# One core, a two-layer denoise step: u's reordering and two loads of Y move from GpSimd's queue to the sync engine's

## The reference, cut to what matters

```python
u, z = split(h @ w_in)                        # 2048 -> 2 x 2048
h_t  = a * h_(t-1) + B u_t                    # complex scan over 128 rows, both directions, 128 groups of 16 channels
y    = gelu(C h + d_skip * u)
y    = y * sigmoid(y @ w_glu + b_glu)
x    = x + gate * ((y * silu(z)) @ w_out)
```

## Time and profile before

| | us |
|---|---|
| median of 3 runs | 1235.92 |
| the three runs | 1229.36, 1235.92, 1236.2 |
| the profiled execution's own time | 1229.89 |
| its span | 1228.1 |

### The profile page before, as it was taken

How to read it: one execution, slowest core, us unless ns; L and a number is a source line. 1 busy time by engine, 2 the same in 40 slices (tenths; PEclk the granted TensorE clock), 3 DMA queues, 4 the chain that set the end, 5 groups by cost and what they waited for, 6 DMA issues and landing times.

```text
span 1228.1 us, 17478 instructions
## 1 busy us (share of the span) xinstructions
PE 1111.2 (90%) x6802; PEld 840.4 (68%) x6802; DVE 766.0 (62%) x1302; ACT 571.1 (47%) x802; POOL 215.5 (18%) x386
## 2 busy tenths in 40 slices
PE   3899998999999999998999979999688977799995
PEld 0356776777777776787777657788577756587884
DVE  4246764766576657666788664299586884365664
ACT  5233443343444344445433454664858466344443
POOL 2001220333022402130322131311010210100000
PEclk9698999999999999999999979999798999899998
DMA  9999785889798978864898867686373946754551
GB/s 355 421 401 398 245 322 196 331 319 345 274 337 323 349 275 328 320 230 174 316 341 339 307 248 272 192 278 227 120 233 120 292 140 221 277 178 162 175 205 70
DMA packets 60035, 327.21 MB, mean 266 GB/s; under 512 B 8801, under 2 KB 11617, under 8 KB 27953
## 3 DMA queue, kind: packets, MB, share of 16 engines
q1 hardware_dynamic: 38816, 262.44, 57.5%
q0 software_dynamic: 14224, 53.16, 12.9%
q10 hardware_dynamic: 6912, 10.49, 2.4%
HBM read 295.65 MB, written 30.41 MB: 265 GB/s over the span
## 4 chain that ended last, share of the span: by engine, by line
PE 68%; DVE 13%; DMA 8%; ACT 6%; issue 3%; SPq 0%; ACTq 0%; POOL 0%; DVEq 0%
PE ps L765 18%; PE ps L766 17%; PE ps L767 17%; PE ps L650 6%; DVE wlo L1449 4%; DVE sb L1556 3%; DMA araw<-in_wada 3%; DVE t L1551 2%; ACT whi L1052 2%; DMA raw<-in_w 2%; PE ps L750 1%; PE ps L880 1%; PE ps L726 1%; PE ps L709 1%; DMA raw<-in_wada 1%
## 5 line engine op out<-in xcount | busy, mean ns | idle before, releaser
L1449 DVE TENSOR_TENSOR wlo<-raw,whi 128x1024 fp32r<-128x1024 f32 x288 | 351.9, 1226 | 373.4 <-ACT whi L1052 369.9
L1052 ACT ACTIVATE whi<-raw 128x1024 fp32r<-128x1024 f32 x288 | 303.0, 1058 | 472.4 <-PE ps L767 458.8
L765 PE MATMUL ps<-whi,xhi 128*128 128x512 f32 x1152 | 478.0, 415 | 5.1 <-DVE xlo L1468 3.8
L766 PE MATMUL ps<-wlo,xhi 128*128 128x512 f32 x1152 | 455.8, 396 | 0.0
L767 PE MATMUL ps<-whi,xlo 128*128 128x512 f32 x1152 | 455.1, 395 | 0.0
L765 PEld LDWEIGHTS ps<-whi,xhi 128*128 128x128 f32 x1152 | 220.4, 191 | 86.3 <-issue 28.7
L767 PEld LDWEIGHTS ps<-whi,xlo 128*128 128x128 f32 x1152 | 219.9, 191 | 49.2
L766 PEld LDWEIGHTS ps<-wlo,xhi 128*128 128x128 f32 x1152 | 220.7, 192 | 46.0 <-issue 4.1
L650 PE MATMUL ps<-araw,cT 128*32 128x512 f32 x640 | 83.4, 633 | 5.0 <-DMA araw<-in_wada 5.0
L1556 DVE TENSOR_TENSOR sb<-sb,t 128x128 f32<-128x128 f32 x256 | 69.0, 290 | 6.6
L880 PE MATMUL ps<-utf,btab 64*128 64x64 f32 x512 | 35.4, 293 | 17.4 <-ACT sb L1145 17.4
(11 more groups left out here) (210 smaller groups left out, 1028.6 us busy)
## 6 DMA issues: line engine op xcount, KB each, us to landing
raw<-in_w SPq DMA_DIRECT2D x144, 1024.0 KB, 5.5
araw<-in_wada SPq DMA_DIRECT2D x80, 1024.0 KB, 8.6
raw<-in_wada SPq DMA_DIRECT2D x16, 1024.0 KB, 9.1
ctab_scratch<-ce POOLq DMA_DIRECT2D x16, 512.0 KB, 8.3
btab_scratch<-bs ACTq DMA_DIRECT2D x32, 256.0 KB, 4.6
btab<-btab_scratch SPq DMA_DIRECT2D x16, 512.0 KB, 4.6
ctab<-ctab_scratch POOLq DMA_DIRECT2D x16, 512.0 KB, 4.9
par<-in_par POOLq DMA_DIRECT2D x32, 128.0 KB, 6.2
```

The source lines that it names most:

```text
L765: mm(acc, xhi[:, kt, st], whi[:, s, k], start=kt == 0, stop=False)
L766: mm(acc, xhi[:, kt, st], wlo[:, slot, k0 % 2, k], start=False, stop=False)
L1052: af(whi[:, k % 4].rearrange("p k c -> p (k c)"), src, ACT.Copy).then_inc(s_hi, 1)
L1449: tt(wlo[:, slot, k % 2].rearrange("p k c -> p (k c)"), src, whi[:, k % 4].rearrange("p k c -> p (k c)").bitcast(F32), ALU.subtract).then_ ...
```

## The change

SyncE stores and loads u. It does this for group w behind the weight chunk 87 + 4w, with the same waits as before: for ScalarE's copies (now one for each stream), for the stores' landing, and for the emptied buffer. For w = 0 it also waits for the last modulation result (`s_adaout`), which GpSimd's program order implied before. SyncE also loads Y of groups 2 and 3, behind the weight chunks 117 and 120. GpSimd keeps Y of groups 0 and 1 and everything else; it waits for ScalarE to have taken u of group 0 before it loads the first local table. It no longer waits for Y's stores of groups 2 and 3, so the loads behind them stand one behind the other with their own waits only. ScalarE waits for `s_factors` in its first `s5_ordered`.

```diff
--- before.py
+++ after.py
@@ -363,6 +363,11 @@
             i = e % 4
             return (raw[:, 2 + i], s_raw[2 + i]) if i < 2 else (araw[:, i - 2], s_araw[i - 2])
 
+        def load_y(eng, w):
+            eng.wait_ge(s_yout, 64 * (w + 1))
+            cols = slice(w * BN, (w + 1) * BN)
+            eng.dma_start(Y[:, :, cols], y_d[:, cols].rearrange("(s p) c -> p s c", s=NS)).then_inc(s_yin[w], 16)
+
         def chain(eng, s):
             n = [0]
 
@@ -390,6 +395,22 @@
                     sp.wait_ge(s_S, n - 3)
                 sp.dma_start(btab[:, n % 4].rearrange("p r i c -> p (r i c)"),
                              bt_d[n // 4, :, n % 4 * 4 * 2 * P:(n % 4 + 1) * 4 * 2 * P]).then_inc(s_bt[n % 4], 16)
+
+            def chunks_of_u(w):
+
+                for st in range(NS):
+                    sp.wait_ge(s_evA, NS * (B_OUT0 + w) + st + 1)
+                    sp.dma_start(u_d[st * P:(st + 1) * P, w * BN:(w + 1) * BN], ub[w % 2][:, st]).then_inc(s_ubout[w % 2], 16)
+                sp.wait_ge(s_ubout[w % 2], 32 * (w // 2 + 1))
+                if w == 0:
+                    sp.wait_ge(s_adaout, fins(B_END))
+                else:
+                    sp.wait_ge(s_u2p, 2 * w)
+                for gh in range(2):
+                    for st in range(NS):
+                        src = u_d[st * P:(st + 1) * P, w * BN:(w + 1) * BN]
+                        sp.dma_start(u2[gh * M2 + st:(gh + 1) * M2:NS],
+                                     src.rearrange("(k t) (e g c) -> k t e g c", t=CH, e=2, g=2)[:, :, :, gh]).then_inc(s_u2, 16)
 
             for g in range(B_END * NCK):
                 b, u = place(2 * g)
@@ -410,6 +431,11 @@
                     sp.wait_ge(s_wused, 2 * (g - 3))
                 slot = w_slot(g)[0]
                 sp.dma_start(raw[:, slot], d["w"][b, :, c]).then_inc(s_raw[slot], 16)
+                for w in range(NW):
+                    if g == NCK * (B_IN1 + w + 1) + 3:
+                        chunks_of_u(w)
+                    if w >= 2 and g == (Y_AT[w] + 8 - w % 2 * 2) // 2 + 2:
+                        load_y(sp, w)
                 if g == 7:
                     for c in range(2):
                         sp.wait_ge(s_ada0, A_EARLY * NCK - 1 + c)
@@ -580,52 +606,23 @@
                         pool.dma_start(kd[p0:p0 + S5C],
                                        band_d[w, :, :, e].rearrange("q j c k -> c (q j) k")[:, :, k0:k0 + 64]).then_inc(s_kd, 16)
 
-            def store_u(w):
-                wait_evacuated(pool, B_IN1 + w)
-                for st in range(NS):
-                    pool.dma_start(u_d[st * P:(st + 1) * P, w * BN:(w + 1) * BN], ub[w % 2][:, st]).then_inc(s_ubout[w % 2], 16)
-                pool.wait_ge(s_ubout[w % 2], 32 * (w // 2 + 1))
-
-            def load_u(w):
-
-                if w >= 1:
-                    pool.wait_ge(s_u2p, 2 * w)
-                for gh in range(2):
-                    for st in range(NS):
-                        src = u_d[st * P:(st + 1) * P, w * BN:(w + 1) * BN]
-                        pool.dma_start(u2[gh * M2 + st:(gh + 1) * M2:NS],
-                                       src.rearrange("(k t) (e g c) -> k t e g c", t=CH, e=2, g=2)[:, :, :, gh]).then_inc(s_u2, 16)
-                pool.wait_ge(s_u2, 64 * (w + 1))
-
-            def load_y(w):
-                pool.wait_ge(s_yout, 64 * (w + 1))
-                cols = slice(w * BN, (w + 1) * BN)
-                pool.dma_start(Y[:, :, cols], y_d[:, cols].rearrange("(s p) c -> p s c", s=NS)).then_inc(s_yin[w], 16)
-
-            for w in range(NW):
-                store_u(w)
-                load_u(w)
-                if w == 1:
-                    local_table(0)
-                    c_table_quarter(0)
-                    c_table_quarter(1)
-            for n in range(2, 8):
+            pool.wait_ge(s_u2p, 2)
+            local_table(0)
+            for n in range(8):
                 c_table_quarter(n)
-                if n % 4 == 1:
+                if n == 5:
                     local_table(n // 4)
             pool.wait_ge(s_S, 4 * NW)
-            load_y(0)
+            load_y(pool, 0)
             for n in range(8, 12):
                 c_table_quarter(n)
             local_table(2)
-            load_y(1)
+            load_y(pool, 1)
             for n in range(12, 16):
                 c_table_quarter(n)
             local_table(3)
-            load_y(2)
             pool.wait_ge(s_hy, 12)
             pool.dma_start(X[:].rearrange("p s c -> p (s c)"), x_keep).then_inc(s_back, 16)
-            load_y(3)
             pool.wait_ge(s_y, 4 * NW)
             pool.dma_start(bglu[:], d["b_glu"].partition_broadcast(P)).then_inc(s_vec, 16)
             pool.wait_ge(s_hy, 16)
@@ -1115,6 +1112,8 @@
             def s5_ordered(w):
 
                 act.wait_ge(s_u2, 64 * (w + 1))
+                if w == 0:
+                    act.wait_ge(s_factors, 1)
                 if w >= 1:
                     act.wait_ge(s_uT, 2 * w)
                 for e in range(2):
```

## The result

| | kernel before | changed kernel |
|---|---|---|
| median of 20 runs | 1231.35 us (1228.02 to 1236.2) | 1236.53 us (1234.11 to 1240.44) |
| ratio to before, 95% interval | | 1.0038 [1.0026, 1.005] |
| span of the profiled execution | 1228.1 us | 1236.6 us |
| mean granted clock | 0.958 | 0.951 |

The change makes the kernel slower by 0.4%, 4.7 us by the ratio. 1231 had been predicted, from a sum of -3 us. The time lies in the range, but on the other side of no change.

The account below looks back on a forecast made before the run. TensorE, 90% busy, was taken as the bound; -6 (u, group 0) + 0 + 3 (Y, group 3) = -3 us gave 1226.9 from the profiled run or 1232.9 from the median, so 1231 was predicted, range 1222 to 1240.

Parts of the forecast that it names:

- sum of -3 us: Whole kernel: -6 for u of group 0, 0 for Y of group 2, +3 for Y of group 3.
- u of group 0: TensorE's 5.6 us wait before u's transposes falls to 0.3, transposes regain 0.94: 6 us gained, bounds 6.5 gain to 2.0 loss.
- u of groups 1 to 3: SyncE storing and loading u for the later groups: no gain and no cost, weight chunk 92 issued about as before.
- the prediction's signs of being wrong: ScalarE's weight splits: no wait on raw expected at groups 1 to 3; wrong if raw waits exceed 13 us in all.
- Y of group 2: TensorE's wait for Y there: 0 change, bounds 0 and 3 us, as ScalarE's next split leaves 3.2 us of slack.
- Y of group 3: 4 MB of bulk loads go ahead of Y's stores, Y lands at 1059: 3 us lost, bounds 0 to 10.8.
- The prediction's slower rival: Y of group 3 lands later than 1062 behind the bulk; with a 14.9 us store landing net +4.8 us; chance 0.17.
- two lots: Base time: runs shown before lie at 1229.4 and about 1236 us, the profiled one in the lower; 1231 chosen between 1226.9 and 1232.9.

Follow-up runs that it names:

- the half alone: Kernel before, with only u's stores and loads moved to SyncE and all of Y loaded by GpSimd in the old order: ratio 0.9946, 6.6 us less.
- The last experiment: Kernel before, with only the 2 MB gate_keep store moved behind u of group 0's store and loads on GpSimd's queue: ratio 0.9936.
- order only: Kernel before, with GpSimd issuing the X reload ahead of Y of group 2 and bglu, gates, gfin ahead of Y of group 3: ratio 1.0114.
- the Y half: Kernel before, with only Y of groups 2 and 3 loaded by SyncE, GpSimd not waiting for their stores, u on GpSimd: ratio 1.009.

## Why the prediction was wrong, by its own steps

**u of group 0: right.** -6 forecast, -6.5 in the profiled pair and -6.6 with the half alone. The steps were close: stores landed at 753.5, which is 752.3 without the 1.2 us by which this execution runs late (754 forecast), and TensorE waited 0.41 (0.3). The loads took 4.8 us to issue and not 2.5, so chunk 88 went out at 758.3 and landed at 764.0. What had been bounded by that chunk was bounded by it. The last experiment adds what the sum did not claim: the cause was the place behind `gate_keep`, not the engine. The microsecond or two that come back before Y were not in the sum.

**u of groups 1 to 3: right.** SyncE issued chunk 92 at 785.03, beside 785.33 before, and no wait for u appears. Two of the prediction's signs of being wrong did show: splits waited for `raw` at groups 1 to 3 (1.32, 1.98, 1.78 and 3.50 us), and the waits on it are 20.8 us in all, above 13. They are covered, as the forecast's zero cost has it: TensorE is busy for 50.0 of the 50 us from 800 to 850, and idle for 0.4 of the 60 before. As signs they were badly chosen, since an idle ScalarE costs nothing here.

**Y of group 2: the size was off.** 0 was taken, with bounds of 0 and 3, and it cost 2.7 us. Y's load took 10.6 us behind chunk 117 and beside X (forecast at most 8.1). The slack of 3.2 us was about right: the transposes of Y started at 1025.17, 5.6 us later than the 1019.6 that 1023.02 less the shift of 3.4 would be, and 2.7 of that reached the outputs.

**Y of group 3: the failing step.** +3 was taken and +9.1 measured. The prediction had the mechanism, bulk of 4 MB ahead of Y's stores, and nearly the moment at which the queues fall empty: 1058.5 forecast, 1058 in the windows, though Y's own 0.5 MB was in that sum and had not been issued yet. Two things failed. The stores were priced at a landing of 5.4 us, the median of all transfers of that scratch, and 15.91 is what the last of them took. The row with 14.9 us entered only a bound, as a worst case. It was the nearest row: that landing is of group 1's last store, where GpSimd's queue moved 2.1 MB beside the four. Their median there is 9.0, and it is the last store that Y's load waits for. And the bytes of stores and load were put into one sum, as if both could be under way at once. Y's load starts when its stores have landed, so the stores wait out the bulk, to 1060.89, and the load's 3.59 us come behind that. The prediction's slower rival, with 14.9 and 6.67 us, is what happened, but for a load that was faster on empty queues. It had been given 0.17 with the argument that at 440 GB/s all bytes are through by 1059. The bulk and the stores nearly were, and Y's load was still to come.

**The base.** The prediction saw two lots in the three runs before and put 1231 between them. The 20 runs of before spread over 1228.02 to 1236.2 with no gap wider than 1.4 us, around 1231.35, so there are no two lots. The sum of -3 us on that median is 1228.3, and 1236.53 was measured. That 1231 lies within the range says little.

**The sentence of the Trainium skill** (DMA: Bandwidth & Descriptors, section Issuing engines are not separate DMA queues) that starting transfers from several engines only saves issue time held in both halves: "order only" (1.0114) loses like the Y half (1.009), and "gates stored after u" (0.9936) gains like the u half (0.9946), without anything moved.

## What to carry to other kernels

When a wait is taken out of an in-order queue, list what stood behind it there, as it will now be issued earlier: here a wait for Y's stores had been holding 4 MB of loads out of the way of these very stores. Price a group of small transfers by the last landing they had beside the same company, not by the median, and add a store and the load that depends on it one after the other, never as one pool of bytes. Before moving a transfer to another engine, try moving the bulk behind it in the same queue.

## What the hardware showed

With long and short packets at work together in the changed kernel, the DMA engines passed one packet of each queue in turn: 287 packets of 11.0 KB against 277 of 0.94 KB over 10 us, and 58, 59 and 60 of three queues over 3 us of it. The queue of short packets got a share of the bytes as small as its packets: 0.26 MB beside 3.15 MB in the same 10 us. That shortening the bulk's packets alone helps the stores was not isolated. Bulk loads cut into pieces of 16 and 32 partitions with rows of 8 and 16 KB kept the engines' share near 1 at 147 to 175 GB/s, where the whole loads had moved 403 to 408.
